# State space of a layer: the gated norm of a group moved into the next group's turn, and the step sizes put ahead of a convolution

## The reference, cut to what matters

```
proj = u @ in_w                                  # z | x, B, C | dt
xbc = silu(causal_depthwise_conv(xbc, conv_w, conv_b))
dt = softplus(dt_raw + dt_bias);  a = dt * -exp(a_log)
y = ssd_chunked(xs * dt, a, B, C)                # 8 groups of 4 heads, 4 chunks of 128 tokens
y = y + d_skip * xs
g = y * silu(z)                                  # the gate
gg = g * rsqrt(mean(g * g over the 256 of a group) + 1e-6)    # the norm of a group
y = gg * norm_w;  return y @ out_w
```

## Time and profile before

| what | value |
|---|---|
| median of 3 runs | 1804.21 us (1804.2 to 1807.23) |
| the profiled execution | 1802.27 us |
| its span, first to last instruction | 1800.5 us |
| TensorE busy | 1726.6 us, 96% |
| VectorE, ScalarE, POOL busy | 865.9, 769.1, 746.6 us |
| mean granted clock of TensorE | 0.984 of full speed |
| share of the 16 DMA engines, weights' queue | 21.9% |

### The profile page before, as it was taken

The page is one execution under the profiler, slowest core; times in us unless marked ns, Lnnn a source line. Parts: engine busy times, 40 slices in busy tenths (PEclk is TensorE's granted clock), DMA queues, the critical chain, the costliest instruction groups (busy, mean ns, idle before and its releaser), DMA issues.

```text
span 1800.5 us, 23493 instructions
## 1 busy us (share of the span) xinstructions
PE 1726.6 (96%) x9056; PEld 1392.2 (77%) x9056; DVE 865.9 (48%) x1773; ACT 769.1 (43%) x1315; POOL 746.6 (41%) x1009
## 2 busy tenths in 40 slices
PE   8999799999999999998988999999999999999998
PEld 7876567977988888887866777777778778787876
DVE  6358963533632222225645664355553544545456
ACT  6545543542642323213444455245443553434443
POOL 5735222232255555542444555555451342323330
PEclk9999799999999999999988999999999999999999
DMA  8522001122132222221121112221221211212201
GB/s 301 177 90 76 18 1 47 48 71 70 48 117 94 94 94 94 98 89 60 70 71 47 57 62 94 71 73 54 85 72 60 72 49 49 84 61 83 83 1 48
DMA packets 25815, 136.51 MB, mean 76 GB/s; under 512 B 2623, under 2 KB 7999, under 8 KB 12008
## 3 DMA queue, kind: packets, MB, share of 16 engines
q1 hardware_dynamic: 25704, 135.02, 21.9%
HBM read 132.88 MB, written 2.12 MB: 75 GB/s over the span
## 4 chain that ended last, share of the span: by engine, by line
PE 80%; DVE 8%; ACT 7%; POOL 2%; issue 2%; DMA 1%; DVEq 0%; ACTq 0%; POOLq 0%; SPq 0%
PE ps L1377 78%; PE ps L1381 2%; ACT whi L1849 1%; POOL wlo L2759 1%; DMA raw<-wall 1%; ACT tmp L1849 1%; DVE mx L2274 1%; ACT L1849 1%; DVE XS L2271 1%; ACT ESG L1849 1%; DVE tmp L2271 1%; POOL ECG L2790 1%; DVE LG L2271 1%; ACT ECG L1849 0%; DVE GY L2271 0%
## 5 line engine op out<-in xcount | busy, mean ns | idle before, releaser
L2759 POOL TENSOR_TENSOR wlo<-raw,whi 128x256 fp32r<-128x256 f32 (+1 forms) x924 | 671.4, 765 | 866.0 <-ACT whi L1849 866.0
L1377 PE MATMUL ps<-XH,whi 128*128 128x512 f32 (+1 forms) x1144 | 301.6, 384 | 9.1 <-ACT XH L1849 9.1
L1849 ACT ACTIVATE whi<-raw 128x2048 fp32r<-128x2048 f32 (+4 forms) x135 | 231.3, 1718 | 174.2 <-PE ps L1377 165.4
L1377 PE MATMUL ps<-XL,whi 128*128 128x512 f32 (+1 forms) x1144 | 281.5, 368 | 0.0
L1377 PE MATMUL ps<-XH,wlo 128*128 128x512 f32 (+1 forms) x1144 | 280.2, 367 | 0.0
L1377 PEld LDWEIGHTS ps<-XH,whi 128*128 128x128 f32 x1144 | 200.5, 190 | 54.8 <-issue 10.3
L1377 PEld LDWEIGHTS ps<-XL,whi 128*128 128x128 f32 x1144 | 203.5, 190 | 36.5
L1377 PEld LDWEIGHTS ps<-XH,wlo 128*128 128x128 f32 x1144 | 203.2, 190 | 35.8
L2363 DVE TENSOR_TENSOR R<-ps,R 128x512 f32<-128x512 f32 (+1 forms) x128 | 79.9, 624 | 261.0 <-PE ps L1377 260.2
L1377 PE MATMUL ps<-BH,whi 128*128 128x512 f32 (+1 forms) x480 | 131.5, 390 | 1.2 <-ACT BH L1849 1.2
L1377 PE MATMUL ps<-BL,whi 128*128 128x512 f32 (+1 forms) x480 | 125.1, 376 | 0.8 <-DVE BL L2686 0.8
(11 more groups left out here) (308 smaller groups left out, 2732.6 us busy)
## 6 DMA issues: line engine op xcount, KB each, us to landing
raw<-wall SPq DMA_DIRECT2D x107, 1024.0 KB, 4.8
raw<-wall SPq DMA_DIRECT2D x11, 512.0 KB, 3.5
raw<-wall SPq DMA_DIRECT2D x8, 576.0 KB, 3.7
raw<-wall SPq DMA_DIRECT2D x4, 768.0 KB, 4.1
BFL<-scr SPq DMA_DIRECT2D x2, 1024.0 KB, 7.0
outT<-R SPq DMA_DIRECT2D x16, 128.0 KB, 1.8
MEM<-memT SPq DMA_DIRECT2D x2, 512.0 KB, 5.0
XTA<-x SPq DMA_DIRECT2D x2, 512.0 KB, 9.6
```

The lines of the kernel that those rows point to most:

```text
L1377: return nc.tensor.matmul(o_, l, r_, start=start, stop=stop, skip_group_check=True)
L1849: return nc.scalar.activation(o_, i_, func, bias=bias, scale=scale)
L2759: t = tt(wlo[u % NSPL][:, c], raw[u % NRAW][:, c], f32(whi[u % NSPL][:, c]), ALU.subtract)
```

## The change

Only the planner's list is changed. No instruction is added, taken away or reshaped.

1. For g = 1, `dc0` is emitted before the last half tile of `xs` instead of after it, `dc1` after that half tile, and `group_end(0)` after one more half tile, the first of `bc`.
2. `scans` no longer has `g2`, `g3`, `g4` nor its two empty steps. These three are a generator of their own, `gated(g)`. The new `turn(g)` weaves them, for group g-1, between the scan steps of group g. So the turn of g now holds the scan of g-1 and the tail of g-2. The turn of 7 holds two tails, 5 and 6; the last one is as before.
3. The ratios change from 1.2 to 1.4 (g = 1), 1.1 (2, 3, 4, 6) and 1.35 (7).
4. In group 5 the four `so` units come between `bc` and `z` instead of ahead of `xs`, in the weight array too.

```diff
     for g in range(8):
-        if g == 5:
-            ssm_out(0, 8)
         for key, cols in [("xs", ...), ("bc", ...), ("z", ar(256 * g, 256 * g + 256))]:
+            if g == 5 and key == "z":
+                ssm_out(0, 8)
...
                 emit("g0", g, c)
                 yield
                 emit("g1", g, c)
-                if c < 3:
-                    return
-                yield
-                emit("g2", g)
-                yield
-                emit("g3", g)
-                yield
-                emit("g4", g)
-
-            for _ in range(2):
-                yield
             chunks = [chunk(c) for c in range(4)]
             for c in range(5):
                 for i in (c, c - 1):
                     if 0 <= i < 4:
                         next(chunks[i], None)
                         yield
-            yield from chunks[3]
+        def gated(g):
+            return chain(*(emits(kind, g) for kind in ("g2", "g3", "g4")))
+
+        def pauses(n):
+            yield from range(n)
+
+        def turn(g):
+            tail, scan, pause = gated(g - 1), scans(g), pauses(2)
+            for part in (tail, pause, scan, scan, pause, tail, scan, tail, *(scan for _ in range(5))):
+                next(part)
+                yield

         token_turn("f", group_in(0), 8)
         for g in range(1, 8):
             main = group_in(g)
             if g == 1:
-                for _ in range(4):
+                for _ in range(3):
                     next(main)
                 emit("dc0")
+                next(main)
                 emit("dc1")
+                next(main)
                 group_end(0)
-            if g == 5:
-                weave(chain(*(project("so", 2, 8, 0) for _ in range(4)), main), scans(g - 1), 0.6)
+                weave(main, chain(pauses(1), scans(0)), 1.4)
+            elif g == 5:
+                beside = turn(4)
+                weave(chain(project("xs", 2, 8, 5), project("bc", 2, 8, 5)), (next(beside) for _ in range(8)), 1.0)
+                weave(chain(*(project("so", 2, 8, 0) for _ in range(4)), project("z", 2, 8, 5)), beside, 0.3)
+            elif g == 7:
+                weave(main, chain(turn(6), gated(6)), 1.35)
             else:
-                weave(main, scans(g - 1), 1.2)
+                weave(main, turn(g - 1), 1.1)
             group_end(g)
-        weave(chain(*(project("so", 2, 6, 1) for _ in range(4))), scans(7), 1.9)
+        weave(chain(*(project("so", 2, 6, 1) for _ in range(4))), chain(pauses(2), scans(7), gated(7)), 1.9)
```

More of the change, by code:

```diff
@@ L1197, in scans, with emits @@
                         yield
-            yield from chunks[3]
+        def emits(*step):
+            emit(*step)
+            yield
[7 more added lines that the diff above has]
+                next(part)
+                yield
         token_turn("f", group_in(0), 8)
@@ L1203, in program @@
             if g == 1:
-                for _ in range(4):
+                for _ in range(3):
                     next(main)
                 emit("dc0")
+                next(main)
                 emit("dc1")
+                next(main)
                 group_end(0)
-            if g == 5:
-                weave(chain(*(project("so", 2, 8, 0) for _ in range(4)), main), scans(g - 1), 0.6)
+                weave(main, chain(pauses(1), scans(0)), 1.4)
[5 more added lines that the diff above has]
+                weave(main, chain(turn(6), gated(6)), 1.35)
             else:
-                weave(main, scans(g - 1), 1.2)
+                weave(main, turn(g - 1), 1.1)
             group_end(g)
-        weave(chain(*(project("so", 2, 6, 1) for _ in range(4))), scans(7), 1.9)
+        weave(chain(*(project("so", 2, 6, 1) for _ in range(4))), chain(pauses(2), scans(7), gated(7)), 1.9)
         between(half_out("so", 1, 8, 2), [rms_norm("r1", j) for j in range(2)] + [1.6], half_in(("cq", "cq")))
-        def emits(*step):
-            emit(*step)
-            yield
         weave(project("cq", 2, 8), emits("lt", 0), 0.9)
```

## The result

The changed kernel took 1820.38 us (median of 4 runs, 1818.8 to 1824.41), beside 1804.2 us for the kernel before on the same chip (4 runs, 1801.81 to 1807.23). The ratio is 1.0091, 95% interval 1.0075 to 1.0107: **slower by 0.9%**. The profiled execution spans 1817.6 us at a mean granted clock of 0.981 (before: 1800.5 and 0.984).

A forecast was written before the change was run, and what follows sets the result against it. TensorE, busy 1726.6 of 1800.5 us, was taken as the bound, so only its pauses could change. Turn terms gave +4.3 us, half clock +16: 1822.6 profiled, 1824.5 median; forecast 1814 to 1834, range 1801 to 1838.

The forecast's parts named there:

- chain of 15.6 us: Plain turns, from the end of bc4 through convolution, norm, BH, whi, POOL's eight subtractions and XDE to TensorE's release.
- Rival B: POOL's block of subtractions is not late, so the stalls and their half clock vanish: 1793 us, faster; chance 0.14.
- four stalls: Turns 2, 3, 4 and 6: TensorE waits 4.7 us at g1.2 for ECG2, behind POOL's eight subtractions.
- the pause at the end: Before group 7's gate: a stall of about 4 us, 0.9 for BH, then the gate; the end +3.2 us.
- rival A: The stall is there but the clock stays up: 1808.5 us, up to 1814 with some drops; chance 0.16.
- the one of 6.8 us in the second turn: Half-rate stretch in the kernel before, TensorE at work 966.69 to 972.50: 2.9 us lost, the price per stall.
- the wait for BH: Turn 5, second half tile of so: BH at 33.5 us, TensorE at 31.5, so +2.0 us.
- my counter-example: Kernel before: 3.08 us of idleness ahead of 1424.61 us with full clock afterwards.
- The pause of the gate: Turn 1: TensorE waits about 2.9 us at 915.6, only two half tiles standing before the first scan step.
- The waits of 2.2 and 1.3 us: Turn 1, after the gate: g1 waits 2.2 us for ESG, the third scan 1.3 us for POOL.
- The pause of 0.91 us before the transposes: TensorE's wait before its transposes, counted as gone in turns 2, 3, 4 and 6.

The follow-up runs named there:

- e1: The changed kernel with the previous group's norm step (g4) one half tile later in turns 2, 3, 4 and 6, so whi precedes the BH copies: 1807.81 us.
- e2: The changed kernel with g0 of chunk 2 emitted ahead of the second weight split in turns 2, 3, 4 and 6, whi still behind the BH copies: 1806.86 us.
- e4: The changed kernel with g0 of chunk 2 and the previous group's g4 exchanged in turns 2, 3, 4 and 6, around the second split: 1797.1 us.
- e5: The kernel of e4 with the norm of group 3 emitted one weave step earlier in turn 5, ahead of the output projection reading it: 1794.36 us.
- e6: The kernel of e5 with turn 7's ratio at 1.5 instead of 1.35, so group 6's tail ends before the last half tile: 1798.76 us.
- e10: The kernel of e9 with the norm's reciprocal-root tile gr in a PSUM bank instead of an SBUF temporary: 1789.73 us.
- e3: The kernel before with only the step sizes and group 0's end moved; each group's tail stays in its own scan's turn: 1803.38 us.
- e8: The changed kernel with dc0, dc1 and group_end(0) in their old places, two empty steps and ratio 1.27 in turn 1: 1830.78 us.
- e9: The kernel of e5 with turn 7's order written by hand, group 6's last two tail steps before the last half tile: 1792.29 us.
- e7: The kernel of e6 with turn 1's scan steps laid out by hand over seven half tiles: 1801.47 us.

## Why the prediction was right, and where its terms were not

**The mechanism, and its place: shown.** The prediction let ECG2 release TensorE 44.0 us into the turn; in turn 4 it came at 1091.75 − 1047.72 = 44.03. The chain of 15.6 us was 15.3 (1076.46 to 1091.75), and its links were the ones named, BH, `whi`, eight subtractions, XDE. TensorE was there at 39.7 instead of 39.3, so the stall was 4.3 and not 4.7 us. e1 took out one link, e2 the other, e4 both, and e4 brought all of it back. At full clock a plain turn was to last 49.5 us; measured are 51.11 with a stretch of 1.6 us lost in it, 49.5. Rival B (1793 us if POOL's block is not late) is not what the change does, but its price was good: e4, the same kernel with the block not late, took 1797.1 us, and with turn 5 mended as well 1794.4.

**The clock: right in kind, mis-sized.** Half rate followed each of the four stalls and the pause at the end, as forecast, and rival A is out. But I had priced a stretch at 2.9 us, from the one of 6.8 us in the second turn. Most of the new ones lasted half as long. The trace of the kernel before had one of these too, ahead of group 1's products, which the earlier trace rows leave out; it is the first row here, and the second is turn 3 of the changed kernel:

```profile
948.70:952.05 3.35, 2.87 (x4) 1.00 (x4) 1.46 (x2) 0.97 (x2) 3.35 (x5) 0.50 0.00 0
...
1041.31:1044.73 3.42, 3.42 (x15) 2.54 (x12) 0.42 (x1) 0.00 (x0) 0.43 (x1) 0.50 0.44 184
```

3.4 us of work at half rate are 1.7 us lost; the turns of e1 with and without one differ by 1.6. In turn 2 (its stretch was 6.8 us, but 2.3 of these fell into the pause), in turns 3, 4 and 6 and at the end that makes 2.2 + 3 × 1.6 + 1.7 = 8.7 us, where five times 2.9, 14.5, were forecast. In turn 1 it was 0.1 instead of 1.5 (below). Sizing every stretch by one row of 6.8 us, with rows of 10.2 and 3.4 us beside it in the same trace, was the weak step.

**The clock where it wasn't counted.** Two stretches came where I had none. In turn 5 the wait for BH was priced well (TensorE's delay from 1130.98, where the next products were due, to 1133.06 is 2.1 us against 2.0), but I gave it no half rate since it was short; it got one, and the turn became 4.1 us longer. The other is my counter-example, behind the state space: the same pause of 3.08 us, with the same instructions, had full clock behind it before and this now:

```profile
1440.29 0.84 PE L1387 MATMUL ps<-PMT,VV 128*128 128x128 f32 x4 [3.08 <-DVE PMT L2731]
...
1440.67:1444.09 3.42, 3.42 (x11) 2.75 (x10) 2.02 (x9) 2.54 (x6) 0.51 (x1) 0.50 0.02 5
```

In the profiles of all ten experiments a half-rate stretch stands at this place too. One row with the clock up was one outcome of two, and not evidence that pauses of 3.1 us are safe.

**Turn 1.** The forecast (−7.6 with the clock) and the measurement (−7.5) agree by two misses that cancel. The pause of the gate came as said, 2.85 us against 2.9, with half rate behind it:

```profile
920.37 0.44 PE L1391 MATMUL ps<-KT,XS 128*128 128x128 f32 x2 [2.85 <-ACT ZS L1859]
...
926.48 0.66 PE L1387 MATMUL ps<-ESG,XDT 128*64 128x128 f32 x8 [0.44 <-DVE ESG L2662]
```

The waits of 2.2 and 1.3 us that were to follow it were 0.44 and 0.66. The first is short only because TensorE, at half rate, came later to it. In e2, e5, e6 and e10 turn 1 has the same steps and the same pause of 2.85 us, but full clock behind it; there this wait is 2.0 us, close to the forecast, as here in e5:

```profile
925.37 0.44 PE L1393 MATMUL ps<-KT,XS 128*128 128x128 f32 x2 [2.85 <-ACT ZS L1861]
...
931.47 0.66 PE L1389 MATMUL ps<-ESG,XDT 128*64 128x128 f32 x8 [2.01 <-DVE ESG L2664]
```

From products to products the turn took 35.15 to 35.17 us in those four and 35.26 in the changed kernel. So the wait absorbed nearly the whole stretch, 0.1 us was lost and not 1.5. (In e4 the stretch lasted 6.8 us, and the turn 36.46.) Against this stands that the turn began 1.6 us late, since `dc0` stood at 901.53 and not at 899.9, for a reason that has nothing to do with the edit (below). Without both, the gain is 9.2 us where 9.1 were forecast. It needs both edits: from the same place, e3 won 1.7 us of it in turn 1 and e8 1.4.

**Turns 2 and 7 and the end.** Full-clock parts of −2.2, +0.7 and +2.7 us against −2.1, +1.3 and +3.2. The pause of 0.91 us before the transposes went in the plain turns, as forecast. e9 shows the end's part to be the place of group 6's tail, since moving that alone gave it back.

**The sum.** At full clock +4.3 was forecast and about +3.6 came (−9.2 −2.2 +2.8 +2.8 +2.5 +3.5 +0.7 +2.7, each a difference of the table less the half rate in it and, in turn 1, less the late start). For the clock +16 was forecast and about +13.4 came: 8.8 where it was counted, 1.6 in turn 5, 1.4 behind the state space, 1.6 ahead of turn 1. The mechanism of the stall and its length were right by reasoning. That the clock's sum is off by 2.6 us and not by 7 is luck: three stretches that I had not counted made good 4.6 us of what the counted ones fell short. Without these three the time would have been some 1816 us, near the lower end of the forecast.

## What to carry to other kernels

When a step is moved in a list that several engines play in order, write out each engine's queue around its new place: here the exchange of two neighbouring steps was worth some 21 us, on engines that are idle more than half the time, because a weight split of 1.9 + 6.4 us stood between a small product and TensorE. Put what TensorE waits for next ahead of the long blocks that are needed much later, and the work whose reader is far away behind them; then look what VectorE does beside POOL's blocks. And move single steps: a ratio shifts a whole turn (e6), a new spread of its scan steps does so too (e7), and each lost more at another place of the turn than it won.

## What the runs showed of the hardware

**VectorE and POOL contend for operands in SBUF, and both get slower.** Eight subtractions of 128x256 on POOL took 5.6 us where VectorE read one operand from SBUF or none, 6.2 to 6.4 beside the scan's small products, and 8.0 to 8.2 beside the norm's two products and two BL subtractions; the pair of products took 1.42 us before and 2.0 to 2.9 there. With one operand in PSUM the pair took 1.39 us again and the block, with BL alone beside it, 7.3. The Trainium skill (SBUF — State Buffer, Who interferes with whom) says that a VectorE instruction with two SBUF inputs contends with a GpSimd instruction that reads SBUF, and one with at most one SBUF input, outside its two-port modes, doesn't; the runs agree with both halves. I had used this rule to choose between 5.6 and 6.2 us, and had not seen that the mended orders would meet it at 8.2.

**The same pause has not always the same clock behind it.** Besides the pause of 3.08 us, there is one place ahead of the state space with identical instructions in all kernels (pauses of 3.2, 0.4, 1.2 and 1.2 us around 840 us in the kernel before): the half-rate stretch there lasted 6.83 us in the kernel before, e1 and e4, 10.24 us in the changed kernel and six others, and 13.65 us in e2 and e8. The 3.4 us more are 1.7 us lost, which is what made the changed kernel reach `dc0` 1.6 us late. In e1 two pauses of 1.92 us had a stretch behind them and two had not. The gate's pause of 2.85 us in turn 1 had one of 3.4 us in the changed kernel, e1 and e9, one of 6.8 us in e4, and none in e2, e5, e6 and e10; the pause of 3.2 us at the end had none in e4 and 6.8 us in e5. A forecast can give such a stretch a chance, and here 1.6 us, less where a wait behind it absorbs it, but not its presence. What decides it stays open: no run varied it.

**The start varies too.** TensorE's first thousand products were through at 201.6 to 202.3 us in seven of the twelve profiled executions and at 204.5 to 205.1 in five (e4, e5, e7, e8, e10), with the same instructions up to there. So the profiled spans of two kernels can differ by 3 us before the first edited line, and by 5.7 with the stretch above; turn lengths, with the same order and the same clock, mostly repeat within 0.1 us. Why the start varies was not tried.
